# Two of eight chunks of a 31-tap convolution on GpSimd, the other sums in PSUM, and split weights for all sixteen glu units

## The reference

```python
h = rmsnorm_2(x, norm1_g)
z = h @ w_in + b_in
z_glu, z_rx, z_rg, z_ga, z_gb = split(z)              # 2048, 1280, 1280, 1024, 1024 columns
u = z_glu[:, :1024] * sigmoid(z_glu[:, 1024:])
u = causal_depthwise_conv(u, conv_dw_w, conv_dw_b)    # 31 taps, each channel by itself
u = silu(layernorm(u, conv_ln_g, conv_ln_b))
y_a = u @ conv_w_out + conv_b_out
xb = causal_depthwise_conv(z_rx, lru_conv_w, lru_conv_b)   # 4 taps
hb = rg_lru(xb, ...)                                  # two gates, a linear recurrence over the tokens
y_b = (hb * gelu(z_rg)) @ lru_w_out
x = x + (sigmoid(z_ga) * y_a + sigmoid(z_gb) * y_b) @ w_mix_out
# then a gated MLP and a last norm
```

## Time and profile before

| | |
|---|---|
| median of 3 runs | 1025.4 us |
| the profiled execution | 1026.5 us |
| its span, first to last instruction | 1024.6 us |
| mean granted clock of PE | 0.985 |
| busy: PE, DVE, ACT, POOL | 989.0, 776.7, 545.1, 1.9 us |

### The profile page before, as it was taken

How to read it: one execution, slowest core, us unless ns; L and a number is a source line. 1 busy time by engine, 2 the same in 40 slices (tenths; PEclk the granted TensorE clock), 3 DMA queues, 4 the chain that set the end, 5 groups by cost and what they waited for, 6 DMA issues and landing times.

```text
span 1024.6 us, 19866 instructions
## 1 busy us (share of the span) xinstructions
PE 989.0 (97%) x7850; PEld 938.0 (92%) x7850; DVE 776.7 (76%) x1381; ACT 545.1 (53%) x897; POOL 1.9 (0%) x14
## 2 busy tenths in 40 slices
PE   4799999999999999999999999999999999999996
PEld 1479999999989899999999989898889999999996
DVE  4757976888767777668766889899987887777554
ACT  4248675444655568875544535468116565444343
POOL 0000000000000000000000000000000000000000
PEclk9689999999999999999999999999999999999998
DMA  9997797887464865554655336363445555555631
GB/s 378 421 420 308 280 372 306 310 329 274 132 204 114 304 247 179 192 170 160 213 202 200 125 127 243 112 223 122 162 162 196 178 178 200 198 177 192 205 125 42
DMA packets 35881, 222.29 MB, mean 217 GB/s; under 512 B 3883, under 2 KB 9180, under 8 KB 9436
## 3 DMA queue, kind: packets, MB, share of 16 engines
q1 hardware_dynamic: 35804, 221.22, 59.9%
HBM read 220.13 MB, written 1.07 MB: 216 GB/s over the span
## 4 chain that ended last, share of the span: by engine, by line
PE 88%; DVE 4%; ACT 3%; DMA 3%; issue 1%; SPq 0%; DVEq 0%; ACTq 0%
PE bank L595 23%; PE bank L601 22%; PE bank L596 22%; PE bank L927 11%; PE bank L976 3%; PE s_banks L624 2%; DMA mod_raw<-w_mod 1%; DVE w_lo L1408 1%; ACT w_hi L1047 1%; PE s_banks L976 1%; DMA raw<-weights 1%; DVE mod_raw L1459 1%; ACT ub L1148 1%; PE s_banks L595 0%; PE s_banks L596 0%
## 5 line engine op out<-in xcount | busy, mean ns | idle before, releaser
L1408 DVE TENSOR_TENSOR w_lo<-raw,w_hi 128x1024 fp32r<-128x1024 f32 x268 | 324.9, 1218 | 32.3 <-ACT w_hi L1047 29.9
L1047 ACT ACTIVATE w_hi<-raw 128x1024 fp32r<-128x1024 f32 x268 | 280.0, 1051 | 109.4 <-PE bank L601 103.1
L595 PE MATMUL bank<-xg_hi,w_hi 128*128 128x258 f32 (+1 forms) x1248 | 310.8, 286 | 1.3 <-DVE w_lo L1408 0.8
L596 PE MATMUL bank<-xg_lo,w_hi 128*128 128x258 f32 (+1 forms) x1248 | 306.2, 282 | 0.0
L595 PEld LDWEIGHTS bank<-xg_hi,w_hi 128*128 128x128 f32 x1248 | 236.1, 189 | 6.2 <-issue 5.1
L596 PEld LDWEIGHTS bank<-xg_lo,w_hi 128*128 128x128 f32 x1248 | 236.5, 190 | 0.2
L601 PE MATMUL bank<-xg_hi,w_lo 128*128 128x258 f32 (+1 forms) x1248 | 181.2, 283 | 0.3 <-DVE w_lo L1408 0.3
L601 PEld LDWEIGHTS bank<-xg_hi,w_lo 128*128 128x128 f32 x1248 | 162.9, 190 | 0.8 <-DVE w_lo L1408 0.8
L595 PE MATMUL bank<-hid_hi,w_hi 128*128 128x256 f32 x512 | 123.5, 279 | 0.0
L596 PE MATMUL bank<-hid_lo,w_hi 128*128 128x256 f32 x512 | 123.4, 279 | 0.0
L1811 DVE SCALAR_TENSOR_TENSOR y<-u,vec,y 128x256 f32<-128x256 f32 x240 | 98.5, 480 | 0.2
(11 more groups left out here) (238 smaller groups left out, 1259.5 us busy)
## 6 DMA issues: line engine op xcount, KB each, us to landing
raw<-weights SPq DMA_DIRECT2D x157, 1024.0 KB, 5.0
mod_raw<-w_mod SPq DMA_DIRECT2D x28, 1024.0 KB, 11.5
mod_raw<-w_dots SPq DMA_DIRECT2D x20, 1024.0 KB, 8.6
toep<-bias_by_distance SPq DMA_DIRECT2D x8, 256.0 KB, 5.4
x<-x_in SPq DMA_DIRECT2D x1, 1024.0 KB, 5.0
toep<-bias_by_distance SPq DMA_DIRECT2D x8, 128.0 KB, 3.9
y_out<-yout SPq DMA_DIRECT2D x4, 256.0 KB, 2.5
c_all<-c_row SPq DMA_DIRECT2D x1, 512.0 KB, 14.6
```

The lines of the kernel that those rows point to most:

```text
L595: pe.matmul(dst, hi, r_hi, start=start, stop=False, skip_group_check=True)
L596: pe.matmul(dst, hi, r_lo, start=False, stop=False, skip_group_check=True)
L1047: act.activation(pool_w_hi[:, at, :] if name == "pool" and at < 2 else w_hi[:, at % HL, :], raw[:, slot, (at % 2) * UT * P:(at % 2 + 1) * ...
L1408: ve.tensor_tensor(lo, raw[:, slot, (at % 2) * UT * P:(at % 2 + 1) * UT * P], hi.bitcast(F32), ALU.subtract).then_inc(lo_done, 1)
```

## The change

`GLU_SPLIT` goes from 8 to 16: glu units 8 to 15 leave `NATIVE` and are split and evicted like the first eight. Chunks 6 and 7 of the convolution (`POOL_TAPS` = 2) are done by GpSimd: it waits until ACT has done all eight first taps, and does then for each of 30 taps a product of both chunks (128x512, the weight broadcast over the tokens) into one of two buffers of `pool_prod`, and a sum into `y`. DVE keeps chunks 0 to 5, 180 taps, and their running sums lie in PSUM banks 4, 5 and 7 (`tap_sum`); only the last tap writes to `y`. The first tap of ACT writes there as well. DVE waits for GpSimd's last sum ahead of its sum over `y`. `TAPS_AT` is written anew for glu and for gb and ga. Two waits are added on DVE: a pair of chunks waits for both first taps, and rx for all of `u`.

```diff
-GLU_SPLIT = 8
+GLU_SPLIT = 16
+POOL_TAPS = 2
-LAST_TAPS = (TAPS - 1) * DC
+LAST_TAPS = (TAPS - 1) * (DC - POOL_TAPS)
-TAPS_AT = {"glu": [0, 0, 0, 0, 1, 1, 1, 1] + 5 * [7] + 3 * [4],
+TAPS_AT = {"glu": [0, 0, 0, 0, 0, 1, 1, 1] + 8 * [2],
            "rx": 5 * [3, 0] + 5 * [4] + 2 * [8] + 3 * [5],
            "gates": 5 * [3] + 3 * [5],
-           "gb": [1, 9, 15, 1, 9, 1, 4, 4] + 8 * [6]}
+           "gb": [1, 9, 13, 1, 5, 1, 3, 3] + 8 * [4]}
+            pool_prod = sb("pool_prod", [P, 2, POOL_TAPS, SEQ], F32, part)
+        tap_banks = (banks[4], banks[5], banks[7])
+        def tap_sum(m):
+            if m >= DC - POOL_TAPS:
+                return y[:, m, :]
+            return tap_banks[m // 2][:, SEQ * (m % 2):SEQ * (m % 2 + 1)]
+            pool.wait_ge(pads, 2)
+            def pool_product(k):
+                if k > 2:
+                    pool.wait_ge(pool_tap, k - 2)
+                at = VEC["dw_w"] + DC * k + DC - POOL_TAPS
+                w = vec[:, at:at + POOL_TAPS].rearrange("p (a n) -> p a n", n=1).broadcast_to((P, POOL_TAPS, SEQ))
+                nc.gpsimd.tensor_tensor(pool_prod[:, k % 2, :, :], u[:, DC - POOL_TAPS:DC, k:k + SEQ], w, ALU.mult).then_inc(pool_mult, 1)
+            def pool_add(k):
+                pool.wait_ge(pool_mult, k)
+                if k > 1:
+                    pool.wait_ge(pool_tap, k - 1)
+                dst = y[:, DC - POOL_TAPS:DC, :]
+                nc.gpsimd.tensor_tensor(dst, dst, pool_prod[:, k % 2, :, :], ALU.add).then_inc(pool_tap, 1)
+            pool.wait_ge(ytap_done, DC)
+            pool_product(1)
+            for k in range(1, TAPS):
+                if k + 1 < TAPS:
+                    pool_product(k + 1)
+                pool_add(k)
-                act.activation(y[:, m, :], u[:, m, 0:SEQ], ACT.Identity, bias=col("dw_b", m), scale=col("dw_w", m)).then_inc(ytap_done, 1)
+                act.activation(tap_sum(m), u[:, m, 0:SEQ], ACT.Identity, bias=col("dw_b", m), scale=col("dw_w", m)).then_inc(ytap_done, 1)
-                        ve.wait_ge(ytap_done, m + 1)
+                        ve.wait_ge(ytap_done, 2 * pair + 2)
-                    ve.scalar_tensor_tensor(y[:, m, :], u[:, m, k:k + SEQ], col("dw_w", DC * k + m), y[:, m, :], ALU.mult, ALU.add)\
+                    dst = y[:, m, :] if k == TAPS - 1 else tap_sum(m)
+                    ve.scalar_tensor_tensor(dst, u[:, m, k:k + SEQ], col("dw_w", DC * k + m), tap_sum(m), ALU.mult, ALU.add)\
+                    if v == 0:
+                        ve.wait_ge(u_done, DC)
             ve.wait_ge(tap_done, LAST_TAPS)
+            ve.wait_ge(pool_tap, TAPS - 1)
```

More of the change, by code:

```diff
@@ L393, in build @@
         tap_done = sem("tap_done")
+        pool_tap, pool_mult = sem("pool_tap"), sem("pool_mult")
         act_read = sem("act_read")
```

## The result

The changed kernel takes 1051.97 us (median of 4 runs, 1051.32 to 1052.81) against 1025.43: a ratio of 1.026, with a 95% interval of 1.024 to 1.028. It is slower by 26.5 us. All intervals here go by runs in the faster of the chip's two states; one of experiment 9's six runs, 1090.1 us at a mean granted clock of 0.846, was in the slower one. The profiled execution took 1052.8, its span 1051.0. In this trace everything ahead of glu lies 2.3 us earlier than in that of before: DVE's row behind the last unit of the stage ahead is at 560.4 and not 562.7. Behind the start of gb this trace takes 331.8 us and that of before 329.5, with no new wait of PE, so the whole spans again differ by 26.4. They lie in the last stages, where PE starts 44 or 45 matmuls in 5 us instead of 46 or 47.

A forecast was written before the change was run, and what follows sets the result against it. PE was taken to bound the kernel, with DVE nearly full and able to take its place. 1026.5 - 5.1 (glu) + 34 (PE's late start of gates) = 1055.4, 1054 us in terms of the median; range 1018 to 1078.

The forecast's parts named there:

- The forecast's mechanism: In rx and rg, DVE instructions with two SBUF inputs and GpSimd operations never run together; chance 0.50, 1054 us.
- Glu, 5.1 us: Eight glu units become split, taking 5.1 us off PE's path, with DVE's added work just fitting beside it.
- Taps into PSUM at no cost: DVE's taps writing sums to PSUM cost 0 extra, at most 0.04 us each, 6.4 us over 161 taps.
- Rival 3: PSUM taps are dear and DVE alone becomes the bound; 1029 us at 0.15 us per tap, chance 0.04.
- The waits: DVE's two-input instructions wait for GpSimd, 22.9 us in rx and 19.6 in rg up to the gates' first split.
- The room: Slack hiding DVE's waits before gates: 3.7 us of DVE idling between 638 and 647, and 5.0 at the first split.
- POOL's start and end: GpSimd's 60 operations begin at 613, take 64 us at 1.06 each and are nearly done when gates start.
- The sum over y: Behind ga, DVE has 14.8 us of room before PE takes up this sum, so later waits add nothing.
- rival 4: In rg units behind PE gaps, a lower granted clock adds 0 to 8 us to the forecast; no chance given.
- rival 1: DVE and GpSimd don't hold each other up, leaving only PE's gain: 1020 us (1018 to 1023), chance 0.36.
- Rival 2: DVE and GpSimd share reads piece by piece, slowing each other only while both run: 1023 to 1033 us, chance 0.10.

The follow-up runs named there:

- experiment 9: Changed kernel with the recurrent sum in PSUM, fewer taps in rx and taps put behind the gates' splits: 1022.2 us, 0.995 of the kernel before.
- Experiment 1: Changed kernel without GpSimd's 60 operations and DVE's wait for them, part of the convolution left out: 1021.35 us, 0.995 of the kernel before.
- 2: Changed kernel, complete, with the running sum of the recurrent taps in a PSUM bank instead of SBUF: 1031.4 us, 1.005 of the kernel before.
- 5: Changed kernel with each of GpSimd's 60 operations replaced by a memset of 128x1024, which only writes: 1022.0 us in a single run.
- 6: Changed kernel with GpSimd's products and sums replaced by copies of 128x512, one input each: 1030.4 us in a single run.
- 7: Changed kernel with all running sums in SBUF, GpSimd's part unchanged: 1068.0 us in a single run.
- experiment 8: Changed kernel with GpSimd's operations starting only when DVE has done the last act_lo in rg: 1024.8 us in a single run.
- Experiment 10: Kernel before with all sixteen glu units split, all 240 taps on DVE, sums in SBUF, no GpSimd work: 1031.8 us, ratio 1.007.

## Why the prediction was right or wrong

**The forecast's mechanism held.** 1054 was forecast, 1052 came. Experiments 1, 2, 5 and 6 show exclusion as the cause: it goes when POOL doesn't read (5), it goes for the one instruction whose second input leaves SBUF (2), and it lasts as long as POOL's operation (6). By the rule in the Trainium skill (SBUF — State Buffer, "Who interferes with whom"), two SBUF inputs of DVE meet GpSimd's reads, not its writes. The trace agrees: 1258 ns beside products and sums, 485 beside memsets.

**Glu, 5.1 us.** Right. Rx begins at 606.35 instead of 613.69, 7.3 us earlier of which 2.3 lie ahead of glu: 5.1. DVE was full and did not hold PE up, as summed.

**Taps into PSUM at no cost.** Right: beside rows 6 (473/480/488) stand

```profile
L1845 DVE SCALAR_TENSOR_TENSOR s_banks<-u,vec,s_banks x116: 473/476/489, 580.6 to 727.2; 128x256 f32<-128x256 f32 x116
L1845 DVE SCALAR_TENSOR_TENSOR bank<-u,vec,bank x58: 479/481/490, 728.3 to 764.6; 128x256 f32<-128x256 f32 x58
```

Rival 3 is out with it. The prediction took these taps as safe but never priced that; without the six banks (7) the loss up to gb grows by 12.6 us.

**The waits, 42.5 us forecast, 33.9 measured.** From the second eviction of rx to the gates' first split DVE takes 84.7 us (612.09 to 696.81) instead of 50.8 (619.43 to 670.25 in rows 5). The pair shown takes 10.45 us instead of 5.93: 4.5 more, where 5.5 was forecast. An rg group, from act_lo to act_lo:

```profile
664.32 0.92 DVE L1829 TENSOR_TENSOR act_lo<-rx,act_hi 128x256 fp32r<-128x256 f32 x1
665.15 2.67 DVE L1821 SCALAR_TENSOR_TENSOR newt<-rx,vec,newt 128x256 f32<-128x256 f32 x2
667.86 1.15 DVE L1822 SCALAR_TENSOR_TENSOR rx<-rx,vec,newt 128x256 f32<-128x256 f32 x1
668.93 1.65 DVE L1845 SCALAR_TENSOR_TENSOR s_banks<-u,vec,s_banks 128x256 f32<-128x256 f32 x4
670.50 1.03 DVE L1829 TENSOR_TENSOR act_lo<-rx,act_hi 128x256 fp32r<-128x256 f32 x1
```

is 6.18 us instead of 3.35: 2.8 more, where 3.7 was forecast. Two terms in it were off, in opposite senses. POOL's operation was put at 1.06. Alone, a product is that (1.04) and a sum isn't (1.27), and the two come in 2.34 us (693.27 to 695.62 in experiment 8), 1.17 for each. And a DVE instruction was taken to wait for a whole operation on top of its own 0.40 from start to start, which with 1.17 would be one tap in 1.57. The recurrent taps come 1.2 to 1.4 us apart, at the pitch of POOL's operations beside them, 1.29 (a pair in 2.59, from 665.03 to 667.62 below).

```profile
665.03 1.10 POOL L600 TENSOR_TENSOR pool_prod<-u,vec 128x512 f32<-128x512 f32 x1
666.10 1.44 POOL L608 TENSOR_TENSOR y<-y,pool_prod 128x512 f32<-128x512 f32 x1
667.62 1.10 POOL L600 TENSOR_TENSOR pool_prod<-u,vec 128x512 f32<-128x512 f32 x1
```

One short DVE instruction gets in for each operation of POOL and lengthens it, but by less than its own 0.40: a product from 1.04 to 1.10, a sum from 1.27 to 1.44. So by these rows the two run side by side for some 0.3 us (1.57 less 1.29) in each turn, and the "whole instruction" that the forecast took over from the Trainium skill was too coarse.

**The room, 8.7 us forecast, 2.4 us measured.** Here the step failed in both of its terms.
- The 3.7 us in which DVE idled between 638 and 647 were counted as room. They are the time that ACT takes for newt and act_hi between two DVE steps, so they come along. The changed kernel has them again, 3.6 us in four waits, one of which is:

```profile
645.25 2.36 DVE L1821 SCALAR_TENSOR_TENSOR newt<-rx,vec,newt 128x256 f32<-128x256 f32 x2 [1.07 <-ACT newt L1303]
```

- The 5.0 at the gates was read from the first split. Five taps stand between the first splits, 3.1 us from one to the next, where PE takes 2.3 for a gates unit, so that room shrinks from one to the next. It has to be read at the last split: before, it starts 6.2 ahead of gb (695.08), in the changed kernel 3.8 ahead (719.17), where PE already waits for single splits. The difference, 2.4 us, is all that there was. Before and after:

```profile
688.90 1.22 DVE L1408 TENSOR_TENSOR w_lo<-raw,w_hi 128x1024 fp32r<-128x1024 f32 x1
```

```profile
715.34 1.21 DVE L1441 TENSOR_TENSOR w_lo<-raw,w_hi 128x1024 fp32r<-128x1024 f32 x1
```

**The sum.** -5.1 + 33.9 - 2.4 = +26.4, as measured (gb at 719.17 instead of 695.08, and 2.3 put back). The forecast was -5.1 + 42.5 - 8.7 = +28.7: waits too large by 8.6, room too large by 6.3. It hit because the two nearly cancel, which is luck, and should not be read as a precision of 2 us.

**POOL's start and end.** Forecast 613 and done near the gates; it ran from 610.9 to 691.8, 81 us where 64 were forecast, and was done 5 us ahead of the gates' first split. **The sum over y** starts at 767.85 and PE takes it up at 784.8: 13.3 us of room, where 14.8 were forecast, and nothing used them.

**The clock** (rival 4) fell where PE had waited: it was granted at 0.77 from 661 to 667, behind a wait of 3.9 us, and at 0.59 in the first 4 us of gates, behind one of 5.3:

```profile
698.00:702.00 4.00, 3.87 (x21) 3.90 (x22) 4.00 (x10) 0.00 (x0) 0.00 (x0) 0.59 0.00 0
```

Fifteen matmuls there begin 0.21 us apart, then 0.12: the lower and the higher of the two levels, 1.2 and 2.4 GHz. It adds nothing to the time here, since the fourth unit of gates waits for its split again (0.5 us), and the account above closes without a term for it. Experiment 10, where nothing behind the wait hides it, prices it at 3.2 us.

**Rivals 1 and 2** gave 1020 and 1023 to 1033. Experiment 1 shows that rival 1's sum was right (1021) for a POOL that isn't there; both failed at the one thing on which no row of before could decide. Rival 2 can also be told from exclusion by the lengths: reads shared piece by piece would stretch a long instruction by the same factor as a short one, but beside POOL a recurrent tap takes 2.6 times its length (485 to 1258 ns) and a split of 1.22 us 1.3 to 1.6 times (1.60 to 1.95).

## What to carry to other kernels

Before work goes to GpSimd, list DVE's instructions that would run beside it by their SBUF inputs: here those with two waited for up to one GpSimd operation each, those with one waited for nothing, and moving a running sum into PSUM took an instruction from the first list to the second at no cost. Idle time of an engine is room only if what it waits for doesn't itself wait for that engine, and room over a run of steps is to be read where it is smallest, here at the last of them. When engines hold each other up inside an instruction, compare durations between the traces; the waits don't show it.

## What the runs showed of the hardware

- Beside each other, a DVE tap with two SBUF inputs (485 ns alone) and a POOL operation have a pitch of 1.29 us, and POOL's operations grow a little, from 1.04 to 1.10 and from 1.27 to 1.45. A split of 1.22 becomes 1.6 to 1.95 and makes POOL's operation 0.9 to 1.0 longer (1.04 to 1.90, 1.27 to 2.27). Beside the DVE product of 2.81 us it was POOL alone that was held up (1.04 to 3.76), so neither engine goes first by rule.
- POOL's price, alone, depends on what it does with 128x512 floats: 1.04 us for a product with a broadcast operand, 1.26 for a sum of two tiles, 0.62 for a copy; a memset of twice the size takes 0.95.
- A tap into PSUM costs DVE the same as into SBUF (476 to 481 against 480 ns), and ACT's first tap is a little cheaper there, 560 against 594 ns.
- After PE had waited 8.3 us (experiment 10) its granted clock was 0.50 for 6 us and 0.66 for the next 4, and 3.2 us were lost by it on top of the wait.
